# New SBUF addresses: tensors that TensorE reads start at multiples of 2048 bytes of a partition, h and a 128 bytes behind one

## The chip, the cores and the metric

The kernel runs on one core of a Trainium2 chip. The metric is the device time of one execution in microseconds (us); lower is better. An interval of durations below is in nanoseconds (ns).

## What is computed

One sequence of 512 tokens, width 1024, passes four layers. `first_block` has two layers: a gated-delta-rule mixer with a short convolution, then a sparse-attention mixer (compressed blocks, selected blocks, window), each followed by a squared-ReLU MLP of width 4096. `second_block` has two layers, each with latent attention, a 2-D Fourier branch and a gated merge. Cut to the products that fill the time:

```python
x = x + mixer(rms_norm(x, mix_norm[layer]))
x = x + squared_relu_mlp(rms_norm(x, mlp_norm[layer]), w_up[layer], w_down[layer])
...
p = _rms_norm(x, norm_g[l]) @ w_in[l]
m = sigmoid(g_a + b0) * ((o_a * silu(z_a)) @ w_attn_proj[l]) + sigmoid(g_f + b1) * ((fourier(u_f) * silu(z_f)) @ w_fourier_proj[l])
x = x + m @ w_out[l]
```

All of it is float32 in the reference.

## The kernel before, in words

Everything stays in SBUF, transposed: features on the 128 partitions, the 512 tokens along the partition. A matmul reads two SBUF operands. The stationary one is loaded into the array first (the profile's PEld rows); the moving one is streamed past it (the PE rows), here 512 columns of 4 bytes, 2048 bytes of each partition.

To keep float32 accuracy at the fast element type (float32r), every large product is made of three matmuls, `three` (lines 760 to 762): weights' high part by activations' low part, weights' low by activations' high, high by high, all added into one PSUM bank. The calls are by `gemm` and `token_major`.

```python
mm(out, w_hi, x_lo, start=first, stop=False)
mm(out, w_lo, x_hi, start=False, stop=False)
return mm(out, w_hi, x_hi, start=False, stop=last)
```

- `gemm`: the stationary operand is a 128x128 tile of `w_hi` or `w_lo`, the moving one a row of 512 tokens of `h_hi`/`h_lo` (the normed input), `a_hi`/`a_lo` (the MLP's hidden part and the mixers' outputs), `cn_hi`/`cn_lo` (latents) or `m_hi`/`m_lo` (merged output).
- `token_major`, and the same three lines in the values' and the Fourier stage: the roles are exchanged. The moving operand is 512 columns of `w_hi` or `w_lo`, the stationary one a 128x128 tile of `h`, `cn` or `d` (`d_hi`/`d_lo`, the Fourier branch's inner product).

The weights come in blocks of eight 128x128 tiles through a ring of three slots: SyncE issues the DMA into `raw`, ScalarE rounds it to `w_hi` (L1415), GpSimd subtracts to `w_lo` (L2709), TensorE waits for `w_lo_ready`. The order of TensorE's work is written out by hand in `program_tensor`. Between the gemms stand other matmuls: sums over partitions of squares in plain float32 (L811, and L819 for the norms), transposes (L1172, L1282, L1145), attention scores and values.

Where each tensor lies is set by `place` alone: `put(name, shape, offset)` allocates at a byte offset of the partition and returns the next free one. The tensors are laid one behind the other from the first free byte, rounded up to 64, which in the built program is byte 16,512 (eight times 2048, and 128). `h` and `a` are bases of two 32 KiB regions at the top, 64 KiB below the end and rounded down to 64: `h_hi` and `h_lo` in the first, `a_hi` and `a_lo` in the second. The layers use the room between, from `local`, one after the other for different tensors. A tile of weights is 512 bytes of a partition, a row of 512 tokens is 2048, so that all rows of a tensor have the same remainder by 2048, and all weight tiles the same by 512.

Of the kernel before, what the change touches and what calls it, by code (L numbers as in the profile page):

```python
# [27 lines left out]
P = 128  # L28
T = 512
D = 1024  # L30
KT = D // P
NT = T // P
# [11 lines left out]
MLA_H, MLA_QK, MLA_NOPE, MLA_ROPE = 8, 96, 64, 32  # L44
# [18 lines left out]
def columns(widths):  # L63

    at, out = 0, {}
    for name, width in widths:
        out[name] = (at, width)
        at += width
    return out, at


COMMON, COMMON_N = columns([("ident", P), ("ones", P)])
PHASE0, PHASE0_N = columns([("blk64", P), ("triu", P), ("notyet", P)])
PHASE1, PHASE1_N = columns([("causal", P), ("cmp_mask", NT * N_CMP), ("rot", P), ("cos", T), ("sin", T)])
PHASE2, PHASE2_N = columns([("dft_d", 2 * P), ("cos4", T), ("sin4", T), ("blk64_2", P), ("blk32_4", 4)])
PHASE_N = max(PHASE0_N, PHASE1_N, PHASE2_N)
PARAMS, PARAMS_N = columns([
    ("eps", 1), ("mix_norm", 2 * KT), ("a_log", 1), ("ab_sign", 1), ("dt_bias", 1), ("mlp_norm", 2 * KT), ("final_norm", KT), ("conv", 12 * 4), ("sc_conv", 4 * 3),
    ("o_norm", 1), ("cmp_pos", 16), ("cmp_k_w2", 2 * P), ("cmp_v_w2", 2 * NSA_D),
    ("norm2", LAYERS2 * KT), ("q_latent", LAYERS2 * 2), ("kv_latent", LAYERS2 * 2),  # L80
    ("eps_qk", 1), ("q_nope", LAYERS2), ("q_pe", LAYERS2), ("q_swap", LAYERS2), ("k_head", LAYERS2), ("k_nope", LAYERS2),
    ("merge", LAYERS2 * 2 * KT)])
# [403 lines left out]
def place(nc, c):  # L486

    at = (nc.sbuf_base + 63) // 64 * 64
    top = nc.sbuf_usable_end

    def put(name, shape, offset, dtype=F32):
        size = (4 * int(np.prod(shape[1:])) + 31) // 32 * 32
        assert offset + size <= top, (name, offset + size - top)
        return nc.alloc_sbuf_tensor_at(name, shape, dtype, offset=offset), offset + size


    c.x, at = put("x", [P, KT, T], at)
    c.raw, at = put("raw", [P, RING, TILES * P], at)
    c.w_hi, at = put("w_hi", [P, RING, TILES * P], at, F32R)
    c.w_lo, at = put("w_lo", [P, RING, TILES * P], at, F32R)  # L500
    c.stage, at = put("stage", [P, 3, T], at)
    c.common, at = put("common", [P, COMMON_N], at)
    c.params, at = put("params", [P, PARAMS_N], at)
    c.tiny, at = put("tiny", [P, 64], at)
    c.norm_r, _ = put("norm_r", [P, 2, T], at, F32R)
    c.norm, at = put("norm", [P, 2, T], at)
    at_rstd = at
# [1 line left out]
    c.rope_x, _ = put("rope_x", [P, 3, T], at)  # L509
    c.rstd, at = put("rstd", [P, 2, T], at)  # L510
    c.sq, at = put("sq", [P, 2, T], at)
    at = (at + 63) // 64 * 64
    phase = at
    at += 4 * max(PHASE_N, PHASE0_N + 2 * T)
    at = (at + 63) // 64 * 64
    c.phase0, _ = put("phase0", [P, PHASE0_N], phase)
    c.eg, _ = put("eg", [P, 2, T], phase + 4 * PHASE0_N)
    c.phase1, _ = put("phase1", [P, PHASE1_N], phase)
    c.phase2, _ = put("phase2", [P, PHASE2_N], phase)
    tail = (top - 2 * 32768) // 64 * 64  # L520
    h, a, local = tail, tail + 32768, at
    c.h_hi, _ = put("h_hi", [P, KT, T], h, F32R)
    c.h_lo, _ = put("h_lo", [P, KT, T], h + 16384, F32R)
    c.a_hi, _ = put("a_hi", [P, KT, T], a, F32R)
# [26 lines left out]
    c.gc_row, _ = put("gc_row", [P, T], o)  # L551
    c.e_row, o = put("e_row", [P, T], o)
    c.tok, o = put("tok", [P, 8, 32], o)
    c.egl, o = put("egl", [P, NT, 4], o)
    assert o <= tail, o - tail
    c.S, o = put("S", [P, 4, P], h)
    c.Sd, o = put("Sd", [P, 4, GDN_D], o)
# [13 lines left out]
    c.kcb, o = put("kcb", [P, 2, 2, N_CMP], o)  # L571
    c.vcb, o = put("vcb", [P, 4, NSA_D], o)
    c.stat, o = put("stat", [P, 16, 16], o)
    o1 = o
    c.kc, o = put("kc", [P, 2, 2, 5, KC_ROW], o1, F32R)
    c.kc_hi, c.kc_lo = c.kc[:, 0], c.kc[:, 1]
    assert o <= tail, o - tail
# [33 lines left out]
    c.k2_pe, o = put("k2_pe", [P, 2, T], o)  # L611
    c.k_hi, _ = put("k_hi", [P, 4, T], a, F32R)
    c.q_hi, _ = put("q_hi", [P, 4, T], a + 16384, F32R)
    odd = [put("u_odd_0", [P, 2, T // 2], o)[0]]
    c.q_root, _ = put("q_root", [P, NT, MLA_H], o + 2048)
    o += 4096
    c.head_t, _ = put("head_t", [P, 2, T], a + 16384)
    far, o = put("prob2_far", [P, 2, T], o)
    near = [put(f"prob2_{i}", [P, 2, T], at_rstd + 4096 * i)[0] for i in range(2)]
    c.prob2 = [*near, far]  # L620
    c.nb2, o = put("nb2", [P, 3, 8], o)
    odd.append(put("u_odd_1", [P, 2, T // 2], o)[0])
    c.u_odd = [odd[g // 2][:, g % 2, :] for g in range(FG)]
    o += 2048
    c.k_pe_hi, o = put("k_pe_hi", [P, T], o, F32R)
    c.sig, _ = put("sig", [P, 4, T], local)
    c.probT2, _ = put("probT2", [P, 2, 2, T], a + 8192)
# [2035 lines left out]
def build(nc, in_x, in_weights, in_common, in_phase0, in_phase1, in_phase2, in_params, out):  # L2663
# [5 lines left out]
    with ctx:  # L2669
        c = Core()  # L2670
        c.in_common, c.in_phase0, c.in_phase1, c.in_phase2, c.in_params = in_common, in_phase0, in_phase1, in_phase2, in_params
        place(nc, c)
        c.pairs = [ctx.enter_context(nc.psum_tensor(f"banks{2 * i}", [P, 2, T], F32)) for i in range(4)]
        c.ld_dram, c.inv_dram, c.invT_dram = [nc.dram_tensor(name, [P, BASE * BASE], F32)[:, :]
# [78 lines left out]
```

## Time and profile before

| what | value |
|---|---|
| time before, median of 3 runs | 2096.04 us (2095.89 to 2101.34) |
| the profiled execution: span from its first to its last instruction | 2099.7 us |
| TensorE matmuls (PE), busy | 2076.6 us, 99% of the span |
| weight loads (PEld), busy | 1645.5 us, 78% |
| VectorE, ScalarE, GpSimd, busy | 947.6, 933.3, 759.2 us |
| DMA, mean rate | 85 GB/s |

How to read it: busy is the union of an engine's instructions. The matmuls' ends in the profile are modelled and they overlap, so that a start-to-start distance, not a duration, tells what a matmul takes of TensorE's time. The profiled execution has no time beside its span; it stands 3.7 us (0.2%) above the runs' median.

### The profile page before, as it was taken

To read this page: it belongs to the slowest core of one execution; us is meant where nothing else is said; L and a number is where in the kernel's file an instruction comes from. 1 tells how busy PE (TensorE), PEld (TensorE's weight loads), DVE (VectorE), ACT (ScalarE), POOL (GpSimd) and SP (SyncE) were. 2 spreads that over 40 slices of the span, in tenths; PEclk is the share of its full clock that TensorE was granted. 3 is DMA by queue.
4 is the path that set the end of the run, shared out by engine and by line. 5 is a ranking of instruction groups with operands and counts; after the bars stand their busy time and mean duration, and the time that the engine had idled before them with its cause. 6 is when DMAs were issued, how large, how long until landed. Compare 5 with 4: busy or idle time off the path is not lost.

```text
span 2099.7 us, 28844 instructions
## 1 busy us (share of the span) xinstructions
PE 2076.6 (99%) x11148; PEld 1645.5 (78%) x11148; DVE 947.6 (45%) x1431; ACT 933.3 (44%) x1477; POOL 759.2 (36%) x316
## 2 busy tenths in 40 slices
PE   8999999999999999999999999999999999999999
PEld 5777788888888886668888888778788887877887
DVE  7875552112137256765211212667733354773331
ACT  7642453323236326774322324556742344765231
POOL 3332144444444630003444444344034443402443
PEclk9999999999999999999999999999999999999999
DMA  4442133333332431002333333232022333201232
GB/s 155 134 123 70 45 104 99 92 101 91 94 99 88 146 96 31 2 14 92 100 91 101 91 101 101 74 97 81 12 81 90 91 93 94 85 22 61 91 100 81
DMA packets 62710, 178.96 MB, mean 85 GB/s; under 512 B 17776, under 2 KB 18160, under 8 KB 62592
## 3 DMA queue, kind: packets, MB, share of 16 engines
q1 hardware_dynamic: 47600, 168.04, 26.3%
q10 hardware_dynamic: 14992, 9.22, 1.6%
q8 instruction: 89, 1.46, 0.3%
q14 instruction: 29, 0.24, 0.0%
HBM read 171.97 MB, written 3.70 MB: 84 GB/s over the span
## 4 chain that ended last, share of the span: by engine, by line
issue 48%; PE 34%; POOL 16%; ACT 1%; POOLq 0%; DMA 0%; SPq 0%; DVE 0%
POOL w_lo L2709 16%; PE banks L760 9%; PE banks L762 9%; PE banks L761 9%; PE banks L1282 1%; PE banks L1295 1%; PE banks L1267 1%; PE banks L811 1%; PE banks L1273 1%; PE banks L1239 0%; DMA x<-in_x 0%; PE banks L1330 0%; POOLq L2715 0%; POOLq L2717 0%; PE banks L1331 0%
## 5 line engine op out<-in xcount | busy, mean ns | idle before, releaser
L2709 POOL TENSOR_TENSOR w_lo<-raw,w_hi 128x1024 fp32r<-128x1024 f32 (+1 forms) x312 | 759.0, 2434 | 1322.8 <-ACT w_hi L1415 1322.7
L760 PE MATMUL banks<-h_lo,w_hi 128*128 128x512 f32 (+1 forms) x1408 | 567.0, 403 | 9.3 <-POOL w_lo L2709 9.3
L762 PE MATMUL banks<-h_hi,w_hi 128*128 128x512 f32 (+1 forms) x1408 | 554.7, 394 | 0.0
L761 PE MATMUL banks<-h_hi,w_lo 128*128 128x512 f32 (+1 forms) x1408 | 551.5, 392 | 0.0
L1415 ACT ACTIVATE w_hi<-raw 128x1024 fp32r<-128x1024 f32 (+1 forms) x312 | 327.9, 1051 | 489.4 <-PE banks L762 456.5
L760 PEld LDWEIGHTS banks<-h_lo,w_hi 128*128 128x128 f32 (+1 forms) x1408 | 264.4, 188 | 73.8 <-POOL w_lo L2709 8.7
L761 PEld LDWEIGHTS banks<-h_hi,w_lo 128*128 128x128 f32 (+1 forms) x1408 | 264.5, 188 | 62.2 <-issue 4.8
L762 PEld LDWEIGHTS banks<-h_hi,w_hi 128*128 128x128 f32 (+1 forms) x1408 | 264.3, 188 | 60.7 <-issue 0.7
L760 PE MATMUL banks<-a_lo,w_hi 128*128 128x512 f32 x768 | 304.5, 397 | 0.0
L762 PE MATMUL banks<-a_hi,w_hi 128*128 128x512 f32 x768 | 301.6, 393 | 0.0
L761 PE MATMUL banks<-a_hi,w_lo 128*128 128x512 f32 x768 | 299.8, 390 | 0.0
L2074 DVE TENSOR_TENSOR x<-x,banks 128x512 f32<-128x512 f32 x104 | 71.4, 687 | 341.0 <-PE banks L762 341.0
L762 PEld LDWEIGHTS banks<-a_hi,w_hi 128*128 128x128 f32 x768 | 144.3, 188 | 33.4
L761 PEld LDWEIGHTS banks<-a_hi,w_lo 128*128 128x128 f32 x768 | 144.4, 188 | 33.0 <-issue 1.0
L760 PEld LDWEIGHTS banks<-a_lo,w_hi 128*128 128x128 f32 x768 | 144.5, 188 | 31.3 <-issue 1.3
L2082 DVE SCALAR_TENSOR_TENSOR relu<-banks,norm 128x512 f32<-128x512 f32 x64 | 44.3, 692 | 270.5 <-PE banks L762 259.8
L1530 ACT ACTIVATE stage<-relu 128x512 f32<-128x512 f32 x64 | 40.5, 632 | 208.7 <-DVE relu L2082 208.7
L2053 DVE TENSOR_TENSOR norm<-norm,sq 128x512 f32<-128x512 f32 x49 | 85.7, 1749 | 2.5 <-ACT sq L1489 1.2
L1973 ACT ACTIVATE sig<-sig,params 128x512 f32<-128x512 f32 x32 | 23.2, 726 | 140.6 <-DVE sig L2635 140.6
L2635 DVE TENSOR_TENSOR sig<-banks,norm 128x512 f32<-128x512 f32 x32 | 22.1, 692 | 111.6 <-PE banks L762 111.6
L1821 ACT ACTIVATE prob<-banks,nb 128x128 f32<-128x128 f32 (+3 forms) x128 | 66.2, 534 | 1.4 <-DVE nb L2452 1.4
L2032 DVE TENSOR_TENSOR a_lo<-stage,a_hi 128x512 fp32r<-128x512 f32 x84 | 61.6, 733 | 7.5 <-ACT a_hi L1478 7.3
(365 smaller groups left out, 2466.5 us busy)
## 6 DMA issues: line engine op xcount, KB each, us to landing
raw<-in_weights SPq DMA_DIRECT2D x311, 512.0 KB, 3.6
x<-in_x SPq DMA_DIRECT2D x4, 512.0 KB, 6.2
AT<-row_dram ACTq DMA_DIRECT2D x4, 512.0 KB, 7.6
out<-x SPq DMA_DIRECT2D x8, 256.0 KB, 2.6
eg<-row_dram ACTq DMA_DIRECT2D x8, 128.0 KB, 3.3
phase<-in_phase ACTq DMA_DIRECT2D x1, 706.0 KB, 4.9
phase<-in_phase ACTq DMA_DIRECT2D x1, 704.0 KB, 4.2
ld_dram<-Ld ACTq DMA_DIRECT2D x1, 512.0 KB, 5.4
```

The source lines that it names most:

```text
L760: mm(out, w_hi, x_lo, start=first, stop=False)
L761: mm(out, w_lo, x_hi, start=False, stop=False)
L762: return mm(out, w_hi, x_hi, start=False, stop=last)
L1415: f(c.w_hi[:, b % RING, 0:n], c.raw[:, b % RING, 0:n], ACT.Copy).then_inc(c.w_hi_ready, 1)
L1530: step(f(c.stage[:, split[key] % 3, :], c.relu[:, i % 2, :], ACT.Square))
L1821: ins = f(c.prob[:, i % 4, s, e], c.pairs[bank[key][0] // 2][:, s, e], ACT.Exp, bias=c.nb[:, i % 4, m:m + 1], accum_out=c.nb[:, i % 4, 4 + ...
L1973: f(gate, gate, ACT.Sigmoid, bias=pa["merge"][:, at:at + 1]).then_inc(c.sig_ready, 1)
L2032: tt_op(dst, stage(key, False), hi.bitcast(F32), ALU.subtract).then_inc(c.split_lo, 1)
L2053: tt_op(c.norm[:, slot, :], c.norm[:, slot, :], c.sq[:, i % 2, :], ALU.add).then_inc(c.norm_sum, 1)
L2074: tt_op(c.x[:, m, :], c.x[:, m, :], out[:, :], ALU.add).then_inc(release(key), 1)
L2082: stt(c.relu[:, i % 2, :], product(key)[:, :], 0.0, r, ALU.max, ALU.mult).then_inc(release(key), 1)
L2709: return nc.gpsimd.tensor_tensor(c.w_lo[:, slot, 0:n], c.raw[:, slot, 0:n], c.w_hi[:, slot, 0:n].bitcast(F32), ALU.subtract)
```

## The change

Only `place` is changed. No instruction is added, removed or moved on any engine: apart from tensors' numbers and source lines the two built programs have the same instructions and the same waits in the same order. What differs is the address that each operand has.

- The small tensors (`tiny`, `q_root`, `nb2`, `egl`) and `common` (identity and ones) go to the front. What follows (`x`, `raw`, `w_hi`, `w_lo`, `stage`, then `norm`, `rstd`, `sq`, `params`) starts at a multiple of 2048.
- `local` is rounded up to a multiple of 2048, and so is the start of `kc`.
- The region of `h` and `a` starts at a multiple of 2048 plus `P`, which is 128 bytes.
- In the second block `u_odd_1` comes right behind `u_odd_0`.

```diff
+    def aligned(n):
+        return (n + 2048 - 1) // 2048 * 2048
+
+    c.tiny, at = put("tiny", [P, 64], at)
+    c.q_root, at = put("q_root", [P, NT, MLA_H], at)
+    c.nb2, at = put("nb2", [P, 3, 8], at)
+    c.egl, at = put("egl", [P, NT, 4], at)
+    c.common, at = put("common", [P, COMMON_N], at)
+    at = aligned(at)
     c.x, at = put("x", [P, KT, T], at)
...
     c.stage, at = put("stage", [P, 3, T], at)
-    c.common, at = put("common", [P, COMMON_N], at)
-    c.params, at = put("params", [P, PARAMS_N], at)
-    c.tiny, at = put("tiny", [P, 64], at)
...
     c.sq, at = put("sq", [P, 2, T], at)
+    c.params, at = put("params", [P, PARAMS_N], at)
     at = (at + 63) // 64 * 64
     phase = at
-    at += 4 * max(PHASE_N, PHASE0_N + 2 * T)
-    at = (at + 63) // 64 * 64
+    at = aligned(at + 4 * max(PHASE_N, PHASE0_N + 2 * T))
...
-    tail = (top - 2 * 32768) // 64 * 64
-    h, a, local = tail, tail + 32768, at
+    tail = (top - 2 * 32768) // 2048 * 2048
+    h, a, local = tail + P, tail + P + 32768, at
...
-    o1 = o
+    o1 = aligned(o)
```

The starts in the two built programs, as the remainder of the byte address by 2048:

| tensors | before | now |
|---|---|---|
| `w_hi`, `w_lo` (also `x`, `raw`, `stage`) | 128 | 0 |
| `h_hi`, `h_lo`, `a_hi`, `a_lo` (also `prob`, `probT`, `k_hi`, `q_hi`, `u_f`) | 1984 | 128 |
| `cn`, `m`, `d`, `qkv`, `q`, `keys`, `v`, `q2`, `k2` | 1216 | 0 |
| `norm`, `sq` | 1664 | 0 |
| `common` | 128 | 672 |
| `kc` | 448 | 0 |

## Rows read from the trace of the kernel before

**Rows 1.** The page: busy time, TensorE in 40 slices, its granted clock.
```profile
PE 2076.6 (99%) x11148; PEld 1645.5 (78%) x11148; DVE 947.6 (45%) x1431; ACT 933.3 (44%) x1477; POOL 759.2 (36%) x316
...
PE   8999999999999999999999999999999999999999
...
PEclk9999999999999999999999999999999999999999
```
**Rows 2.** Who waited longest, TensorE, whole span: total us, times, longest.
```profile
PE banks L760 <- POOL w_lo L2709: 9.3, 2, 8.3
PE banks L811 <- ACT sq L1453: 2.3, 2, 2.1
```
**Rows 3.** Line 760, whole span: count, ns min/median/max, first to last start.
```profile
L760 PE MATMUL banks<-h_lo,w_hi x1408: 388/394/801, 8.3 to 2044.1; 128*128 128x512 f32 x175, 128*40 128x512 f32 x1
...
L760 PE MATMUL banks<-a_lo,w_hi x768: 388/394/799, 234.4 to 2049.7; 128*128 128x512 f32 x192
...
L760 PE MATMUL banks<-w_lo,cn_hi x16: 393/394/796, 1412.4 to 1795.3; 128*128 128x512 f32 x16
```
**Rows 4.** Line 762 in 301 to 651 us (first MLP).
```profile
L762 PE MATMUL banks<-a_hi,w_hi x256: 392/392/392, 339.3 to 646.3; 128*128 128x512 f32 x128
L762 PE MATMUL banks<-h_hi,w_hi x254: 392/392/392, 300.9 to 650.4; 128*128 128x512 f32 x127
```
**Rows 5.** Line 762 in 1538 to 1723 us; last row in 1888 to 2097.
```profile
L762 PE MATMUL banks<-h_hi,w_hi x136: 397/397/398, 1538.9 to 1723.0; 128*128 128x512 f32 x136
...
L762 PE MATMUL banks<-a_hi,w_hi x64: 397/397/398, 1550.1 to 1672.6; 128*128 128x512 f32 x64
...
L762 PE MATMUL banks<-m_hi,w_hi x64: 397/397/398, 1673.3 to 1717.4; 128*128 128x512 f32 x64
...
L762 PE MATMUL banks<-m_hi,w_hi x64: 392/397/398, 2050.9 to 2095.0; 128*128 128x512 f32 x64
```
**Rows 6.** Busy by stretch: PE, PEld, DVE, ACT, POOL, clock, DMA share, GB/s.
```profile
400.00:500.00 100.00, 100.00 (x438) 82.07 (x437) 19.30 (x30) 31.47 (x40) 43.37 (x18) 1.00 0.32 96
...
1920.00:2020.00 100.00, 100.00 (x430) 81.01 (x429) 33.48 (x35) 29.07 (x35) 44.34 (x19) 1.00 0.31 95
```
**Rows 7.** Line 762, windows 778.5:783.6 and 1527:1538 (weights moving), 1397:1404.6.
```profile
L762 PE MATMUL banks<-w_hi,h_hi x8: 392/393/398, 778.6 to 783.5; 128*128 128x512 f32 x8
...
L762 PE MATMUL banks<-w_hi,d_hi x15: 394/394/394, 1527.7 to 1537.5; 128*128 128x512 f32 x15
...
L762 PE MATMUL banks<-cn_hi,w_hi x11: 392/392/392, 1397.3 to 1404.1; 128*128 128x512 f32 x11
```
**Rows 8.** Timeline of PE, 1722.5 us on: start us, us, instruction.
```profile
1722.30 0.40 PE L762 MATMUL banks<-h_hi,w_hi 128*128 128x512 f32 x1
1722.53 0.40 PE L760 MATMUL banks<-h_lo,w_hi 128*128 128x512 f32 x1
...
1723.23 1.02 PE L819 MATMUL banks<-norm,common 128*128 128x512 f32 x2
1723.69 0.79 PE L760 MATMUL banks<-h_lo,w_hi 128*128 128x512 f32 x1
```
**Rows 9.** Line 819, whole span.
```profile
L819 PE MATMUL banks<-norm,common x14: 590/591/667, 22.6 to 1723.7; 128*128 128x512 f32 x14
```
**Rows 10.** Timeline of PE, about 12 us: weight tiles of 40 columns.
```profile
12.18 0.39 PE L762 MATMUL banks<-h_hi,w_hi 128*40 128x512 f32 x1
...
13.56 0.40 PE L762 MATMUL banks<-h_hi,w_hi 128*40 128x512 f32 x1
```
**Rows 11.** Lines 761 and 760 in 301 to 651 us.
```profile
L761 PE MATMUL banks<-h_hi,w_lo x255: 388/388/388, 300.7 to 650.9; 128*128 128x512 f32 x128
...
L760 PE MATMUL banks<-h_lo,w_hi x254: 394/394/394, 301.1 to 650.6; 128*128 128x512 f32 x127
```
**Rows 12.** Waits in 301 to 651 us, all engines: total us, times, longest.
```profile
POOL w_lo L2709 <- ACT w_hi L1415: 197.2, 64, 5.7
...
ACT w_hi L1415 <- PE banks L762: 123.2, 31, 4.4
```

More of the change, by code:

```diff
@@ L553, in place @@
     c.tok, o = put("tok", [P, 8, 32], o)
-    c.egl, o = put("egl", [P, NT, 4], o)
     assert o <= tail, o - tail
@@ L613, in place @@
     c.q_hi, _ = put("q_hi", [P, 4, T], a + 16384, F32R)
-    odd = [put("u_odd_0", [P, 2, T // 2], o)[0]]
-    c.q_root, _ = put("q_root", [P, NT, MLA_H], o + 2048)
+    odd = [put(f"u_odd_{i}", [P, 2, T // 2], o + 2048 * i)[0] for i in range(2)]
     o += 4096
@@ L620, in place @@
     c.prob2 = [*near, far]
-    c.nb2, o = put("nb2", [P, 3, 8], o)
-    odd.append(put("u_odd_1", [P, 2, T // 2], o)[0])
     c.u_odd = [odd[g // 2][:, g % 2, :] for g in range(FG)]
-    o += 2048
     c.k_pe_hi, o = put("k_pe_hi", [P, T], o, F32R)
```

## The prediction

> **What bounds the kernel now.** I read the page's busy times first. TensorE is busy 99% of the span at the full granted clock, 2.4 GHz [rows 1]; the reader should see that there is no idle time to win. Then its waits: the longest are a 9.3 us start and 2.3 us [rows 2]. So the time is the number of matmuls times what each takes of TensorE, and an edit of addresses can only act through the second factor. Third, the line of the split product: 1408 with `h` moving, 768 with `a` [rows 3], and five smaller groups, from 128 with `m` down to 16 with weights moving against latents, 248 together. That is 2424 on L760 and as many on L761 and L762, 7272 in all.
>
> Fourth, their start-to-start distance, from counts between first and last starts. In the first MLP 510 L762 matmuls start from 300.9 to 650.4 us, so a triple takes 349.5 / 509 = 0.6866 us, and one matmul **228.9 ns** [rows 4]. In the second block 264 of them start from 1538.9 to 1723.0 us: 184.1 / 263 = 0.700 us, **233.3 ns** each [rows 5]. The clock, GpSimd's, DMA's and ScalarE's load are alike in both rhythms [rows 6], and so are line and operands (`h`, `a` against `w`). The slow rhythm begins where weights are the moving operand: there a triple takes 9.8 / 14 = 0.700 us too [rows 7]. It goes on in the gemms behind, as if it were handed from one matmul to the next, until a norm's plain-float32 pair (L819) breaks in at 1723.23 us [rows 8]. After the same kind of break, with weights moving, it stays slow (4.9 / 7 = 0.700 us [rows 7]; 778.6 us lies just behind such a pair), while with `h` moving the trace goes over to 228.9. Latents moving against weights: 6.8 / 10 = 0.68 us [rows 7]; at 0.1 us of resolution that is the faster rhythm, and their 392 ns is its mark: 388, 392 and 394 ns of the three lines [rows 4, 11] against 397 [rows 5].
>
> Same shapes, same types, same engine state, only other addresses, and another rhythm: that is my evidence that addresses matter by a few ns.
>
> How much could there be? A plain-float32 pass of 512 columns starts 1.02 - 0.59 = 0.43 us before its second [rows 8, 9]. It streams the same 2048 bytes at half the rate, so a pass at the full rate would be 215 ns. The split matmuls take 14 to 18 ns more. That excess is not the load of full weight tiles: with 40-column tiles instead of 128, six matmuls start in 13.56 - 12.18 = 1.38 us, 230 ns each [rows 10].
>
> The Trainium skill (TensorE: Matmul & The Clock Gate, "Wait — 56ns, not 53.3ns?") gives N / 2.4 GHz + 2.5 ns for back-to-back matmuls, 215.8 ns at 512 columns; the trace disagrees for this element type by 13 ns or more. By that page the 7272 matmuls would take 103 us less than they do; it does not tie the difference to addresses.
>
> **The change, part by part.**
> - *Nothing is issued, waited for or transferred differently.* Cost 0.
> - *Work of ScalarE, VectorE, GpSimd and DMA at new addresses:* 0. GpSimd waits 197 us and ScalarE 123 us of these 350 us for others [rows 12], so a few per cent more or less there stay covered. If matmuls got 6% faster, the weights' chain still has that room.
> - *Other matmuls* (transposes, attention, sums; some 3900): 0, since nothing in the trace tells their addresses apart. Bounds: 2 ns each way, 8 us, kept in the range's ends.
> - *The 7272 split matmuls.* Slow ones now: 280 triples in the third layer (the 264 of rows 5, and 16 of the Fourier stage ahead of them), 272 in the same stretch of the last layer, whose last row stands in rows 5 with the same 397 ns, and 48 triples of tokens' values: 600 triples, 1800 matmuls at 233.3. The other 5472 take 228.9. Bounds for what they take after it: 215 ns (the half-rate pass doubled) and 233.3 (the slow rhythm for all).
>
> Which value? Count 128-byte pieces that an operand touches. `h` or `a` moving now covers 17 (it starts 64 behind a piece's edge), a weight tile 4. Weights moving cover 16, a tile of `h`, `cn` or `d` stationary 5. The first pair allows 228.9, the second only 233.3: a stationary operand off the edge seems to cost more than a moving one. After the change every one of them starts on an edge: 16 and 4. At 256 bytes a weight tile goes from 3 pieces to 2, at 512 from 2 to 1; nothing gets worse at any size. So I take an improvement of both rhythms, and a small one: 226 ns, since one of the three lines in the fast rhythm is already at 388 ns, 3 ns under the mean 391 of the three [rows 4, 11]. That value is a choice near the upper end; no row shows 215 for this type.
>
> Sum: 5472 x 2.9 = 15.9 us; 1800 x 7.3 = 13.1 us; together **29 us** off. 2099.7 - 29 = 2070.7 for the profiled execution; the runs' median is 3.7 lower, so **2067 us**. This case's own range: 224 to 228 ns for all, 2053 to 2082.
>
> **Rivals.**
> - *The excess goes.* If it is all the price of starts off 2048, 7272 matmuls fall to 215: 5472 x 13.9 + 1800 x 18.3 = 109 us, 1987. Against it: `h` and `a`, nine tenths of the moving operands, still straddle a multiple of 2048 (at 128 instead of 1984), and a latent row that straddles it elsewhere runs like `h` [rows 7]. Chance 0.10.
> - *Only the slow rhythm goes.* 1800 x 4.4 = 8 us: 2088. For it: 228.9 shows for two different starts of the moving operand, 1984 and 1216, so it may be a floor. Chance 0.12.
> - *No effect, or effects that cancel:* 2096. The rhythm may come from what ran before, not from addresses. The Trainium skill (SBUF — State Buffer, "Who interferes with whom") says that TensorE never waits on another engine and has two independent SBUF read ports, one for each operand; by it the addresses are free. The trace has no other engine's load behind the two rhythms, which agrees, but the two rhythms themselves are outside that rule. Chance 0.17.
> - *Slower: the slow rhythm takes everything.* The one moving operand that now starts 128 behind a multiple of 2048 is the weights', and it ran at 233.3 each time, right after a break too [rows 7]. The change gives exactly that start to `h` and `a`. If the moving start decides, and not the stationary one, 5472 matmuls go up by 4.4 ns: 24 us, **2120**. It decides from a mean above 230.9 ns (the mean is 230.0 now; 6.3 us over 7272 is 0.9). Against it: then latents and merged rows at 0 are untried, and the weights' runs had another stationary operand. Chance 0.24.
>
> **How the numbers follow.** Small gain 0.37, the three rivals on that side and none 0.10, 0.12, 0.17, slower 0.24. A measurement of this kernel tells 0.3%, 6.3 us, from no change. Faster by more: 0.37 + 0.10 + 0.12 = 0.59; within: 0.17; slower by more: 0.24. The range runs from 2010 us, which leaves out the full gain, to 2122, which holds the slow case: it leaves out some 0.15. The likeliest case is worth a third of the chance only, so the sign is far from sure.
>
> **What would show it.** Starts of L762 in the first MLP: 510 in less than 349 us is a gain; 0.678 us per triple is my forecast, 0.700 the slow rival, 0.645 the whole excess. In the second block the same distance as in the first, with no slow stretch. Matmul durations under 392 ns, and under 397 where weights move. Counts in a 100 us stretch: 442 forecast, 430 slow, against 438 and 430 now [rows 6]. TensorE's waits unchanged, and transposes too. I am wrong if the triple's time is unchanged in the MLPs, or if the gain lies in other matmuls.

## The result, and the profile after

The changed kernel takes **2114.11 us** (median of 4, 2113.2 to 2115.09) against 2096.16 us before: ratio 1.0083, 95% interval 1.0068 to 1.0098. It is slower by 0.8%, where I had forecast 2067 us. Executions of the kernel before scatter more than those of the changed one: from 2095.89 to 2101.34 us here, and from 2093.96 to 2107.63 us beside the experiments below. In these runs a time is 1.8 us more than its span (2113.32 us for the changed kernel's span of 2111.5 us), so that the profiled execution of the kernel before, with 2099.7 us, belongs to its slower ones, some 2101.5 us as an estimate.

The page of the changed kernel, parts 1 and 2. The three split lines are now L762, L763 and L764 (before 760 to 762).

```profile
span 2111.5 us, 28844 instructions
...
PE 2092.9 (99%) x11148; PEld 1647.8 (78%) x11148; DVE 949.3 (45%) x1431; ACT 933.3 (44%) x1477; POOL 757.7 (36%) x316
...
PEclk9999999999999999999999999999999999999999
```

TensorE is busy 16.3 us longer with the same number of matmuls at the same clock [rows 1]. The span is 11.8 us longer, less than the 18 us between the medians, for the reason just given. The view of TensorE's waits still has hardly anything in it but the start [rows 2]:

```profile
PE banks L762 <- POOL w_lo L2711: 8.4, 2, 7.7
PE banks L1161 <- ACT prob L1823: 1.2, 2, 0.8
```

So each matmul takes longer. The last line of the triple in the first MLP, changed kernel (count, ns min/median/max, first to last start):

```profile
L764 PE MATMUL banks<-a_hi,w_hi x256: 390/393/404, 339.4 to 651.0; 128*128 128x512 f32 x128
L764 PE MATMUL banks<-h_hi,w_hi x247: 390/393/404, 301.0 to 606.4; 128*128 128x512 f32 x124
```

503 triples start from 301.0 to 651.0 us: 350.0 / 502 = 0.697 us, 232.4 ns a matmul, where [rows 4] gave 228.9. The same reading of the third layer, whose stretch begins with the Fourier product, and of the latents (windows 1541:1551.5, 1555:1736 and 1410:1418.5 us):

```profile
L764 PE MATMUL banks<-w_hi,d_hi x14: 389/389/397, 1542.0 to 1550.9; 128*128 128x512 f32 x14
...
L764 PE MATMUL banks<-h_hi,w_hi x133: 392/392/398, 1555.1 to 1735.8; 128*128 128x512 f32 x133
...
L764 PE MATMUL banks<-a_hi,w_hi x64: 392/395/398, 1564.2 to 1686.7; 128*128 128x512 f32 x64
L764 PE MATMUL banks<-m_hi,w_hi x64: 389/389/393, 1687.4 to 1730.2; 128*128 128x512 f32 x64
...
L764 PE MATMUL banks<-cn_hi,w_hi x13: 389/389/389, 1409.7 to 1417.9; 128*128 128x512 f32 x13
```

Here the answer stands in one view. `m` against weights takes 42.8 / 63 = 0.679 us a triple, 226.5 ns a matmul, and was at 233.3 [rows 5]. The Fourier product (8.9 / 13 = 0.685 us, 228 ns, 389 ns in duration) was at 233.3 too [rows 7]. Latents take 8.2 / 12 = 0.683 us, which at 0.1 us of resolution can't be told from the 0.68 us before [rows 7]; their duration fell from 392 to 389 ns. These three are what got moving and stationary starts at the same remainder. `h` and `a`, which stand 128 bytes off the weights, have 392 to 398 ns and stay slow: 176 starts from 1564.2 to 1686.7 us, 122.5 / 175 = 0.700 us, 233.3 ns a matmul here where the first MLP has 232.4.

The bookkeeping agrees. The first transposes of the probabilities in the third layer mark how far the kernel has come. Before, then changed (L1282 became L1284), whole span:

```profile
L1282 PE MATMUL banks<-common,prob x176: 270/273/329, 1467.6 to 1897.1; 128*128 128x128 f32 x176
```

```profile
L1284 PE MATMUL banks<-common,prob x176: 270/273/331, 1481.9 to 1911.1; 128*128 128x128 f32 x176
```

The changed kernel is 14.3 us late at the first and 14.0 us at the last, and 11.8 us at the end of the span. All is lost before 1468 us, where the kernel before ran in its faster rhythm; from there on it breaks even, and the merged rows bring some back. Transposes themselves are unchanged, 273 ns.

### The profile page after: what moved, and what is told of

It reads as the page before. It is cut to its first block, busy times and chain, and to the rows that moved or that the text cites. A ratio compares the mean times of both kernels' runs of the same rounds, so it can differ in the third digit from the quotient of the medians.

```text
span 2111.5 us, 28844 instructions
## 1 busy us (share of the span) xinstructions
PE 2092.9 (99%) x11148; PEld 1647.8 (78%) x11148; DVE 949.3 (45%) x1431; ACT 933.3 (44%) x1477; POOL 757.7 (36%) x316
## 4 chain that ended last, share of the span: by engine, by line
issue 48%; PE 34%; POOL 16%; ACT 1%; POOLq 0%; DMA 0%; SPq 0%; DVE 0%
POOL w_lo L2711 16%; PE banks L762 9%; PE banks L764 9%; PE banks L763 9%; PE banks L1284 1%; PE banks L1297 1%; PE banks L1269 1%; PE banks L813 1%; PE banks L1275 1%; PE banks L1241 0%; DMA x<-in_x 0%; PE banks L1332 0%; POOLq L2717 0%; POOLq L2719 0%; PE banks L1333 0%
## 5 line engine op out<-in xcount | busy, mean ns | idle before, releaser
L762 PE MATMUL banks<-h_lo,w_hi 128*128 128x512 f32 (+1 forms) x1408 | 569.1, 404 | 8.4 <-POOL w_lo L2711 8.4
L764 PE MATMUL banks<-h_hi,w_hi 128*128 128x512 f32 (+1 forms) x1408 | 556.7, 395 | 0.0
L763 PE MATMUL banks<-h_hi,w_lo 128*128 128x512 f32 (+1 forms) x1408 | 556.4, 395 | 0.0
L762 PEld LDWEIGHTS banks<-h_lo,w_hi 128*128 128x128 f32 (+1 forms) x1408 | 264.7, 188 | 78.2 <-issue 8.2
L763 PEld LDWEIGHTS banks<-h_hi,w_lo 128*128 128x128 f32 (+1 forms) x1408 | 264.9, 188 | 64.6 <-issue 5.3
L764 PEld LDWEIGHTS banks<-h_hi,w_hi 128*128 128x128 f32 (+1 forms) x1408 | 264.6, 188 | 63.6 <-issue 1.1
L762 PE MATMUL banks<-a_lo,w_hi 128*128 128x512 f32 x768 | 305.0, 397 | 0.0
L763 PE MATMUL banks<-a_hi,w_lo 128*128 128x512 f32 x768 | 303.1, 395 | 0.0
L764 PE MATMUL banks<-a_hi,w_hi 128*128 128x512 f32 x768 | 303.1, 395 | 0.0
L762 PEld LDWEIGHTS banks<-a_lo,w_hi 128*128 128x128 f32 x768 | 144.6, 188 | 34.9 <-issue 1.3
L763 PEld LDWEIGHTS banks<-a_hi,w_lo 128*128 128x128 f32 x768 | 144.6, 188 | 34.7 <-issue 1.0
L764 PEld LDWEIGHTS banks<-a_hi,w_hi 128*128 128x128 f32 x768 | 144.6, 188 | 33.9
```

## Experiments

Two theories stood for the slow-down. **Moving start** (my slow rival): a moving operand that begins 128 behind a multiple of 2048 is slow. **Pair**: what counts is the distance from the start of the stationary operand to that of the moving one, and remainders by 2048 count for nothing. A third, that addresses do nothing and a rhythm is handed on, was the rival "no effect".

Every spacing below is read as above, from counts and starts of the triple's last line in the first MLP, window 305:645. Each ratio is to executions of the kernel before that ran beside that experiment; their median was 2096.02 us beside the runs of the first three sections and the one at 64, and 2101.16 to 2101.46 us beside the others.

### h and a at the weights' remainder

```diff
-    h, a, local = tail + P, tail + P + 32768, at
+    h, a, local = tail, tail + 32768, at
```

> The changed kernel with h and a at remainder 0 by 2048 instead of 128; all else as changed. In its trace h and a against weights start 232.4 to 233.3 ns apart, but latents, merged rows (moving at 0, weights at 0) 226.7 to 227. Pair theory (the distance from the stationary start to the moving start sets the spacing): distance is now 0 everywhere, all 7272 split matmuls at about 227: 6528 x 5.6 ns = 37 us less than the changed kernel, about 2077 us, and faster than the kernel before. Moving-start theory (only the moving start by 2048 counts): the same 2077, since moving starts are 0. Rival, history alone (a rhythm handed on from what ran before, addresses without effect): h and a keep a mean of 229 to 233, 2096 to 2114.

Measured: **2077.64 us** (2076.81 to 2079.93), ratio to the kernel before 0.9912, interval 0.989 to 0.9934. The trace:

```profile
L764 PE MATMUL banks<-a_hi,w_hi x256: 388/389/390, 335.6 to 639.5; 128*128 128x512 f32 x128
L764 PE MATMUL banks<-h_hi,w_hi x245: 388/389/397, 305.0 to 645.0; 128*128 128x512 f32 x123
```

340.0 / 500 = 0.680 us, 226.7 ns. One number of the change, 128, turns a gain of 18 us into a loss of 18. Handed-on rhythm alone is out; the other two both said this.

### The kernel before, only the distance set to 0

```diff
-    tail = (top - 2 * 32768) // 64 * 64
+    tail = (top - 2 * 32768) // 64 * 64 - 320
```

> The kernel before with one number changed: h and a 320 bytes lower, at remainder 1664, so that the distance to weights (at 128) is 1536, a multiple of 512; nothing is aligned to 2048. Pair theory (distance by 512): h and a against weights at about 227 ns as the changed kernel's latents, in place of 228.9 and 233.3: 6528 matmuls x 1.9 to 6.3 ns, 12 to 20 us less, 2076 to 2084. Alignment theory (a start at a multiple of 2048 is what is cheap): no gain, 2096 or more, since every tensor stays off. Moving-start theory: 1664 was not seen with this type; it says nothing of 1664, but would need 227 to be a chance.

Measured: 2082.62 us (2081.47 to 2090.02), ratio 0.9947, interval 0.9926 to 0.9967.

```profile
L762 PE MATMUL banks<-a_hi,w_hi x256: 389/389/389, 338.4 to 642.4; 128*128 128x512 f32 x128
L762 PE MATMUL banks<-h_hi,w_hi x244: 389/389/389, 305.1 to 644.4; 128*128 128x512 f32 x122
```

339.3 / 499 = 0.680 us again, with `h` and `a` at 1664 and weights at 128. No operand of the split products starts at a multiple of 2048 here. The 226.7 ns belong to the distance, and alignment is not needed for them. The time stays 5 us above the run before, where latents, merged rows and the Fourier product were at distance 0 too.

### The pair turned round

```diff
-    at = aligned(at)
+    at = aligned(at) + 128
     c.x, at = put("x", [P, KT, T], at)
...
-    h, a, local = tail + P, tail + P + 32768, at
+    h, a, local = tail, tail + 32768, at
```

> The changed kernel with the pair turned round: h and a at 0, weights (with x, raw, stage, norm, sq) at 128. The distance is minus 128 for h and a, and for latents, merged rows; plus 128 for weights moving. Pair theory: everything is at the changed kernel's 232.4 to 233.3, latents and merged rows too (272 + 128 matmuls more at 5.6 ns, 3 us): 2114 to 2119. Moving-start theory: h, a, latents, m start at 0 and go at 227, weights moving at 233: about 2078.

Measured: **2122.25 us** (2119.3 to 2125.88), ratio 1.0128, interval 1.0102 to 1.0154.

```profile
L764 PE MATMUL banks<-a_hi,w_hi x244: 392/395/398, 340.2 to 644.7; 128*128 128x512 f32 x122
L764 PE MATMUL banks<-h_hi,w_hi x242: 392/395/398, 305.2 to 608.3; 128*128 128x512 f32 x121
```

339.5 / 485 = 0.700 us, 233.3 ns, although `h` and `a` now start at multiples of 2048. This separates the theories: moving start said 2078, pair 2114 to 2119. The median is 3 us above the pair theory's upper end; the profiled execution took 2119.87 us, and the four reach from 2119.3 to 2125.88 us. The spacing in this MLP is 233.3, the upper of the two values that the theory allowed.

### The kernel before, only the distance set to 128

```diff
-    tail = (top - 2 * 32768) // 64 * 64
+    tail = (top - 2 * 32768) // 64 * 64 - 192
```

> The kernel before with h and a 192 bytes lower, at remainder 1792: the distance to weights is 1664, which is 128 by 256, as in the changed kernel, with nothing aligned and everything else as before. Pair theory with period 256: h and a at 232.4 to 233.3, latents, merged rows and weights moving as before (229 to 233): 7272 x 2.6 to 3.3 ns over before, 2115 to 2120. Moving-start theory (a moving start of 128 by 2048 is what is slow): 1792 is no such start, so no slow-down, 2096.

Measured: 2117.15 us (2116.8 to 2118.17), ratio 1.0068, interval 1.0051 to 1.0085; the kernel before stood at 2101.46 beside it.

```profile
L762 PE MATMUL banks<-a_hi,w_hi x244: 392/395/398, 340.3 to 644.8; 128*128 128x512 f32 x122
L762 PE MATMUL banks<-h_hi,w_hi x243: 392/392/398, 304.6 to 608.4; 128*128 128x512 f32 x122
```

340.2 / 486 = 0.700 us. The change's slow-down appears in the old layout without anything aligned or moved to the front, and with a moving start of 1792. That is the change's cause, by itself.

### Other distances

All are the changed kernel with another number in the place of `P`, here for 64:

```diff
-    h, a, local = tail + P, tail + P + 32768, at
+    h, a, local = tail + 64, tail + 64 + 32768, at
```

> The changed kernel with h and a at 64. The distance to weights is 64; it was 1856 before (64 by 256, 320 by 512), with spacings 228.9 or, handed on behind weights moving, 233.3. Pair theory with period 256: the same rhythms as before, 228.9 for h and a, less time in the slow one if the Fourier stage (distance 0 now) no longer starts it: 2114 - 6528 x 3.6 ns = 2090. Pair theory with a longer period: another spacing than 228.9. Moving-start theory with pieces of 128 bytes: 17 pieces instead of 16, not faster than the changed kernel.

> The changed kernel with h and a at 256: distance 256 from the weights' tiles. By distance so far: 0 gives 226.7 to 227.2, 64 228.9, 128 232.4 to 233.3, 320 (before) 228.9 or 233.3, 384 and 448 233.3. Pair theory with period 256: same as distance 0, h and a at 227, about 2078. Pair theory with period 512: 256 is the farthest point from 0 and may stand near 233, 2114 or more. Moving-start theory: no statement.

> The changed kernel with h and a at 192. Period 256: 192 is the class of the weights moving in the kernel before (192 and 448), 233.3 each, so h and a at 233.3: 6528 x 0.8 ns over the changed kernel, about 2119. Period 512 or a rule of the size of the distance: between the values at 128 (232.4) and 256.

> The changed kernel with h and a at 32. If the spacing changes smoothly with the distance: between 227 (0) and 228.9 (64), some 228, about 2084. If it goes in pieces of 64 bytes: like 0, 2078. If 32 off a piece's edge costs one more piece: more than 228.9, over 2090.

> h and a at 96. By distance so far: 0 227, 32 233.3, 64 228.9, 128 232.5, 192 233.3. If odd multiples of 32 are always the bad ones, 233.3 again: 2116. If the distance acts smoothly between 64 and 128, some 230.7: 2102.

| distance of `h`, `a` from weights, bytes | time, us | ratio to before, 95% | us per triple, first MLP | ns per matmul |
|---|---|---|---|---|
| 0 | 2077.64 | 0.989 to 0.9934 | 340.0 / 500 | 226.7 |
| 32 | 2116.45 | 1.0048 to 1.0083 | 339.5 / 485 | 233.3 |
| 64 | 2089.49 | 0.9953 to 0.9978 | 339.9 / 495 | 228.9 |
| 96 | 2118.14 | 1.0054 to 1.01 | 340.2 / 486 | 233.3 |
| 128 (the change) | 2114.11 | 1.0068 to 1.0098 | 350.0 / 502 | 232.4 |
| 192 | 2116.04 | 1.0047 to 1.0081 | 339.5 / 485 | 233.3 |
| 256 | 2077.37 | 0.9861 to 0.9896 | 339.3 / 499 | 226.7 |

The times at 0 and at 256 are the same; their ratios differ because the kernel before stood at 2096.02 us beside the one and at 2101.25 us beside the other.

The rows of the trace at 256, at 32 and at 64:

```profile
L764 PE MATMUL banks<-a_hi,w_hi x256: 389/389/390, 336.4 to 640.4; 128*128 128x512 f32 x128
L764 PE MATMUL banks<-h_hi,w_hi x244: 389/389/390, 305.1 to 644.4; 128*128 128x512 f32 x122
```

```profile
L764 PE MATMUL banks<-h_hi,w_hi x247: 393/394/397, 305.1 to 611.7; 128*128 128x512 f32 x124
L764 PE MATMUL banks<-a_hi,w_hi x239: 393/396/397, 343.6 to 644.6; 128*128 128x512 f32 x120
```

```profile
L764 PE MATMUL banks<-a_hi,w_hi x256: 391/392/393, 336.5 to 643.5; 128*128 128x512 f32 x128
L764 PE MATMUL banks<-h_hi,w_hi x240: 391/392/393, 304.9 to 644.8; 128*128 128x512 f32 x120
```

The reader should see that the remainder by **256** sorts the rows: 256 is 0 again, and 64 gives the spacing of the kernel before, whose distance 1984 - 128 = 1856 is seven times 256 plus 64. It is no smooth curve: 32 and 96 are as bad as 192. Smoothness between 0 and 64 (2084) and between 64 and 128 (2102) was a miss; the third reading at 32 (one more piece, over 2090) and the odd multiples of 32 came true. The remainder does not fix the value to the last ns: at 128 the first MLP has 232.4 in the changed kernel and 233.3 in the two runs above, and the changed kernel itself has both. The kernel before fits in all its parts: weights moving (128) against `h` (1984) or `d` and `cn` (1216) have distances with remainder 192, and ran at 233.3 [rows 7].

The run at 64 also tells of the slow stretch before. There `h` and `a` at remainder 64 ran at 233.3 behind the Fourier product, which stood at remainder 192 [rows 5, 7]. With the same 64 and the Fourier product at 0, the third layer reads (window 1540:1690):

```profile
L764 PE MATMUL banks<-h_hi,w_hi x122: 391/392/393, 1539.7 to 1661.3; 128*128 128x512 f32 x122
L764 PE MATMUL banks<-a_hi,w_hi x64: 392/392/393, 1546.6 to 1666.8; 128*128 128x512 f32 x64
```

127.1 / 185 = 0.687 us, 229.0 ns. So at a remainder where two rhythms are possible, the one that is entered depends on the matmuls before; at 0 none of these traces has `h` or `a` in a slow stretch. The old layout with `h` and `a` at 0 shows that best: there the Fourier product is still at remainder 192 and slow (L762 from 1518.4 to 1528.9 us, 10.5 / 15 = 0.700 us), and right behind it `h` and `a` take 129.3 / 190 = 0.681 us (1530.2 to 1659.5 us).

This may also be why the kernel before scatters, and it is not shown. Its two slow stretches hold 280 and 272 triples; if they ran at 228.9 it would save 552 x 3 x 4.4 ns = 7.3 us, an estimate, which is the step between its executions near 2101 us and those near 2094. With `h` and `a` at 64 and no slow stretch behind the Fourier product, nine executions lie between 2089.2 and 2091.3 us. No trace of a 2094 us execution was taken.

### Only one of the two weight tensors 128 behind

```diff
-    c.w_lo, at = put("w_lo", [P, RING, TILES * P], at, F32R)
+    c.w_lo, at = put("w_lo", [P, RING, TILES * P], at + P, F32R)
...
-    h, a, local = tail + P, tail + P + 32768, at
+    h, a, local = tail, tail + 32768, at
```

> h, a and w_hi at 0, w_lo (with stage, norm, sq) 128 behind. Only line 763's own pair (moving h_hi, stationary w_lo) has the distance minus 128. If what counts is the tile that is loaded while the operand streams, the distance from 762 to 763 (h_lo streams while w_lo is loaded) grows from 227 towards 233 to 240, and 763 to 764 stays. If a matmul's own tile counts, 763 to 764 grows and 762 to 763 stays. In both a triple takes 681 + 6 to 19 ns: 2176 triples x 6 = 13 us or more over the 2078 of h at 0, 2090 to 2100. If only the moving start counts: 2078.

Measured: 2106.70 us (2105.42 to 2109.34), ratio 1.0022, interval 1.0013 to 1.0032. Lines 762, 763, 764 with `h`:

```profile
L762 PE MATMUL banks<-h_lo,w_hi x240: 396/396/396, 304.9 to 603.7; 128*128 128x512 f32 x120
...
L763 PE MATMUL banks<-h_hi,w_lo x240: 397/397/397, 305.1 to 603.9; 128*128 128x512 f32 x120
...
L764 PE MATMUL banks<-h_hi,w_hi x241: 389/389/389, 304.7 to 604.2; 128*128 128x512 f32 x121
```

Where `h` and `a` stream, all moving starts are those of the 2077.64 us kernel, and of the split products' tensors only `w_lo` moved (with `stage`, `norm` and `sq` behind it): 29 us more. Moving start falls once more. Two of three lines grew, from 389 to 396 and 397: L762, during which the shifted tile is loaded, and L763, which uses it. L764 kept 389. The starts say the same: in the mean of this window's triples L763 starts 232.5 ns after L762, L764 starts 234.2 ns after L763, and the next L762 starts 226.7 ns after L764. In the kernel with `h` at 0 the three are 226.4, 226.9 and 226.7 ns. I had expected one of the two; what the runs show is that a shifted load lengthens both matmuls beside it, and they don't say which of the two is held and which only follows. A triple takes 0.693 us here (491 of them, 304.7 to 644.4 us), 13 ns over 0.680; my bounds were 6 and 19. The time is above the 2090 to 2100 us that I had written, because two matmuls of the triple grew and not one.

### Half of each weight tile

```diff
-            w = slice(t * width, t * width + width)
+            w = slice(t * width, t * width + (width if key[0] not in ('up', 'down') else 64))
```

The output's rows are cut to 64 in the same calls.

> h and a at 0, and in the two MLPs only the first 64 of 128 columns of each weight tile are loaded (half of the MLPs' products is left out; the moving side is unchanged). If the 11 ns over 215 that stay at distance 0 come from the load of the tile, half a load gives 221 or less between starts in the MLPs; if the moving stream alone makes them, 227 stays.

> The changed kernel (h and a at 128) with the same half tiles in the MLPs. If the distance acts through the tile's load, the excess over e9 in the MLPs (5.6 ns with full tiles) shrinks to about 3 ns or goes to 0. If the distance acts through the two starts alone (first bytes, once per pair), it stays 5.6 ns.

Measured: 2087.78 us (2087.0 to 2089.63) at distance 0, 2103.60 us (2102.09 to 2108.46) at 128. Lines 764 of the two, in the same window:

```profile
L764 PE MATMUL banks<-a_hi,w_hi x253: 389/397/398, 338.2 to 644.5; 128*64 128x512 f32 x127
L764 PE MATMUL banks<-h_hi,w_hi x240: 389/393/398, 305.0 to 602.4; 128*64 128x512 f32 x120
```

```profile
L764 PE MATMUL banks<-a_hi,w_hi x254: 389/390/397, 338.3 to 644.5; 128*64 128x512 f32 x127
L764 PE MATMUL banks<-h_hi,w_hi x241: 389/390/397, 304.6 to 601.8; 128*64 128x512 f32 x121
```

339.5 / 492 = 0.690 us, 230.0 ns, at 0; 339.9 / 494 = 0.688 us, 229.4 ns, at 128. The first is a miss in both of its branches: half a load made the matmuls *slower* than the 226.7 of full tiles. The second: the 5.7 ns between the distances are gone, while both starts are what they were. So the distance does not act through the two first bytes alone. That fits an effect of the tile's load, but the output's rows are halved along with the tile, and no run separates the two. The excess over 215 ns did not shrink with the bytes that a tile load reads. Where it comes from stays open.

## Why the prediction was wrong

- *What bounds the kernel, and that only the time per matmul can move:* right. Waits, other engines and transposes stayed as they were.
- *The evidence that addresses matter, from the two rhythms:* right, and the size of a change too (some 4 ns per matmul, 1%). Whoever had stopped at "no waits, so no effect" would have missed 18 us.
- *"Count 128-byte pieces that an operand touches ... nothing gets worse at any size":* this is the step that failed. It judged each operand alone. It read the 233.3 ns of weights moving as the price of a stationary tile off an edge. The distance, taken by 256, sorts the same rows better: 192 there, always at 233.3; 64 for `h`, `a`, latents and merged rows, at 228.9 or, handed on, at 233.3. It was in the numbers of the case (1984, 1216, 128), and I had not formed it. The change gives `h` and `a` remainder 128, which no row before had; for such a distance the trace held nothing, and my argument filled the hole with "better". What the runs showed in its place: at 128 bytes between the operands of a matmul the spacing is 232.4 to 233.3 ns, aligned (2114.11 us) or not (2117.15 us), and at 0 it is 226.7 ns, aligned (2077.64 us) or not (2082.62 us).
- *The value 226 ns:* near what the changed kernel has at distance 0 (226.5 for merged rows, 228 for latents and the Fourier product), which is 744 of the 7272 matmuls, less the 96 with weights moving against `h`. For the 6528 with `h` and `a` it is 232.4 to 233.3. In its own terms: the gain of 2.9 ns on each of 5472 matmuls came out as a loss of 3.5 ns where `h` and `a` had been fast, and of the 13.1 us for the slow 1800 only the share of the merged rows, of the Fourier product and of weights moving against latents (4.8 / 7 = 0.686 us, 1427.0 to 1431.8 us) came in.
- *The slow rival, 24 us and 2120:* its size was nearly right (18 us), its mechanism wrong, so that the near hit of 2120 on 2114.11 us is luck. A moving start 128 behind a multiple of 2048 is not what makes it slow: with the moving operand at a multiple of 2048 it was slower still (2122.25), and at 1792 as slow (2117.15). No run had that start together with distance 0.
- *The rhythm that is handed on:* borne out at remainder 64. At remainder 0 it was not: `h` and `a` ran at 0.681 us a triple right behind a slow Fourier product.
- *The rule cited there* (the Trainium skill, SBUF — State Buffer, "Who interferes with whom": TensorE has independent read ports for its two operands and waits for no one) would have left the time as it was. The runs disagree for this element type: moving one of the two stationary tensors by 128 bytes cost 29 us.

## What to carry to other kernels

Where matmuls stream 512 float32r columns and load a new 128-column tile each time, place the moving and the stationary tensors so that their starts have the same remainder by 256; here that was worth 0.9% for all split products (2077.64 against 2096.02 us), 0.5% for `h` and `a` alone in the old layout (2082.62 us), and the wrong distance cost up to 1.3% (2122.25 us). With 64-column tiles this advice was not borne out. Align the pair, not each tensor: starts at multiples of 2048 did nothing by themselves (226.7 ns at distance 0 with them and without). When an engine is 99% busy without waits, take the start-to-start time for each combination of operands: rows that differ in address only are an experiment that the trace has already made.

## What the runs showed of the hardware

- Where `h` and `a` stream against weights, the spacing of float32r matmuls of 512 columns takes few values, by the distance between the two SBUF operands modulo 256: 226.7 ns at 0, 228.9 or 233.3 at 64, 232.4 or 233.3 at 128, 233.3 at 32, 96 and 192.
- No run came near the 215 ns worked out from the plain-float32 pass; 226.7 ns was the least that lasted for `h` and `a`.
- With 64-column tiles in the MLPs the distance hardly matters: 230.0 ns at 0 and 229.4 at 128.
